# Another order of the SBUF buffers in a fp32 transformer kernel of two blocks

## The reference

```python
def swiglu(x, w_gate, w_up, w_down):
    return (jax.nn.silu(x @ w_gate) * (x @ w_up)) @ w_down      # 1024 -> 2816 -> 1024

for l in range(2):
    h = rmsnorm(x, ffn1_norm[l])
    x = x + 0.5 * swiglu(h, ffn1_w_gate[l], ffn1_w_up[l], ffn1_w_down[l])
    h = rmsnorm(x, mix_norm[l])
    p = h @ w_in[l]
    ...
    x = x + jnp.concatenate([y_pool, y_four, y_attn], axis=-1) @ w_out[l]
    h = rmsnorm(x, ffn2_norm[l])
    x = x + 0.5 * swiglu(h, ffn2_w_gate[l], ffn2_w_up[l], ffn2_w_down[l])
```

## Time and profile before

| | us |
|---|---|
| median of 3 runs | 2531.75 |
| lowest and highest run | 2531.56, 2534.13 |
| span of the profiled execution | 2529.9 |
| TensorE busy | 2457.5 |
| GpSimd busy | 1122.4 |
| VectorE busy | 1134.4 |
| ScalarE busy | 1082.3 |

### The profile page before, as it was taken

One profiled execution on the slowest core, in us unless ns is written; L12 is line 12 of the kernel. 1 busy time (PEld: TensorE's weight loads), 2 busy tenths in 40 slices (PEclk: granted clock), 3 DMA queues, 4 the chain that ended last, 5 costly groups with the idle time before them and its releaser, 6 DMA issues.

```text
span 2529.9 us, 30096 instructions
## 1 busy us (share of the span) xinstructions
PE 2457.5 (97%) x10934; PEld 1924.6 (76%) x10934; DVE 1134.4 (45%) x1780; ACT 1082.3 (43%) x1584; POOL 1122.4 (44%) x828
## 2 busy tenths in 40 slices
PE   8999999989999999999999989999999998999988
PEld 6888888667888888888888668888887665676666
DVE  5444115564444105444025655444136655465553
ACT  4333124454333214333132544333125777357772
POOL 4554445415455445554445414554445232352323
PEclk9999999999999999999999999999999999999999
DMA  4222223202222222222223203222233222122212
GB/s 172 85 97 99 100 88 128 84 34 100 99 99 88 95 100 92 91 99 99 100 83 129 73 32 110 90 98 99 100 119 104 83 80 67 67 96 75 84 63 83
DMA packets 37528, 233.17 MB, mean 92 GB/s; under 512 B 5184, under 2 KB 5312, under 8 KB 10816
## 3 DMA queue, kind: packets, MB, share of 16 engines
q1 hardware_dynamic: 36000, 226.51, 25.9%
q10 hardware_dynamic: 1440, 5.45, 0.6%
HBM read 223.55 MB, written 2.10 MB: 89 GB/s over the span
## 4 chain that ended last, share of the span: by engine, by line
issue 58%; POOL 41%; POOLq 1%
POOL w_lo L437 41%; POOLq L431 0%; POOLq L435 0%; POOLq L212 0%; POOLq L437 0%; POOLq L1874 0%
## 5 line engine op out<-in xcount | busy, mean ns | idle before, releaser
L437 POOL TENSOR_TENSOR w_lo<-raw,w_hi 128x512 fp32r<-128x512 f32 x824 | 1122.2, 1394 | 1406.9 <-ACT w_hi L924 1406.8
L445 PE MATMUL ps<-h_hi,w_hi 128*128 128x512 f32 x2304 | 921.3, 400 | 14.0 <-DVE h_lo L1330 7.9
L447 PE MATMUL ps<-h_hi,w_lo 128*128 128x512 f32 x2304 | 900.3, 391 | 0.0
L446 PE MATMUL ps<-h_lo,w_hi 128*128 128x512 f32 x2304 | 899.2, 390 | 0.0
L924 ACT ACTIVATE w_hi<-raw 128x1024 fp32r<-128x1024 f32 x412 | 413.3, 1052 | 881.2 <-PE ps L447 877.0
L445 PEld LDWEIGHTS ps<-h_hi,w_hi 128*128 128x128 f32 x2304 | 434.5, 189 | 115.7 <-issue 13.8
L446 PEld LDWEIGHTS ps<-h_lo,w_hi 128*128 128x128 f32 x2304 | 434.6, 189 | 93.5 <-issue 6.0
L447 PEld LDWEIGHTS ps<-h_hi,w_lo 128*128 128x128 f32 x2304 | 433.7, 188 | 92.2
L447 PE MATMUL ps<-hid_hi,w_lo 128*128 128x512 f32 x704 | 278.1, 395 | 0.0
L445 PE MATMUL ps<-hid_hi,w_hi 128*128 128x512 f32 x704 | 278.1, 395 | 0.0
L446 PE MATMUL ps<-hid_lo,w_hi 128*128 128x512 f32 x704 | 278.1, 395 | 0.0
(11 more groups left out here) (236 smaller groups left out, 2083.6 us busy)
## 6 DMA issues: line engine op xcount, KB each, us to landing
raw<-in_stream SPq DMA_DIRECT2D x206, 1024.0 KB, 4.8
hraw<-xs SPq DMA_DIRECT2D x96, 64.0 KB, 2.0
x_sb<-in_x SPq DMA_DIRECT2D x4, 512.0 KB, 10.5
out_x<-x_sb SPq DMA_DIRECT2D x8, 256.0 KB, 2.7
mem_sb<-in_mem ACTq DMA_DIRECT2D x1, 1024.0 KB, 10.2
rec_sb<-in_recip ACTq DMA_DIRECT2D x2, 512.0 KB, 4.6
memn<-in_mem ACTq DMA_DIRECT2D x1, 1024.0 KB, 4.8
dist_sb<-in_dist ACTq DMA_DIRECT2D x2, 448.0 KB, 3.1
```

What stands on the lines that cost most here:

```text
L437: gp.tensor_tensor(w_lo[:, s, c], raw[:, s, c], w_hi[:, s, c].bitcast(F32), ALU.subtract).then_inc(lo_split, 1)
L445: pe.matmul(dst, l_hi, r_hi, start=first, stop=False)
L446: pe.matmul(dst, l_hi, r_lo, start=False, stop=False)
L447: return pe.matmul(dst, l_lo, r_hi, start=False, stop=last)
```

## The change

The program text of the placement is turned round. The stacks of the shared stage buffers are entered first. Since they are all closed again, a tensor "region" of the size of the hidden layer's two parts (90,112 bytes, as much as any stage needs) is entered behind them to hold their range; nothing reads or writes it. Then come w_hi and w_lo, h_hi and h_lo, x_sb, raw and the small tensors. No instruction, wait, semaphore or loop is changed, and on every engine the instructions stand in the same order as before. Line numbers in the changed kernel are one higher from the PSUM tensor on.

```diff
-        x_sb = sb("x_sb", [P, KB, T])
-        h_hi = sb("h_hi", [P, KB, T], F32R)
-        h_lo = sb("h_lo", [P, KB, T], F32R)
-        raw = sb("raw", [P, 2, PANEL])
-        w_hi = sb("w_hi", [P, 2, PANEL], F32R)
-        w_lo = sb("w_lo", [P, 2, PANEL], F32R)
-        cst = sb("cst", [P, NC])
...
         ffn = ExitStack()
         hid_hi = sb("hid_hi", [P, FB, T], F32R, ffn)
         hid_lo = sb("hid_lo", [P, FB, T], F32R, ffn)
...
         two.close()
+        sb("region", [P, 2 * FB * T])
+        w_hi = sb("w_hi", [P, 2, PANEL], F32R)
+        w_lo = sb("w_lo", [P, 2, PANEL], F32R)
+        h_hi = sb("h_hi", [P, KB, T], F32R)
+        h_lo = sb("h_lo", [P, KB, T], F32R)
+        x_sb = sb("x_sb", [P, KB, T])
+        raw = sb("raw", [P, 2, PANEL])
+        cst = sb("cst", [P, NC])
...
```

More of the change, by code:

```diff
@@ L304, in build, with const @@
         two.close()
+        sb("region", [P, 2 * FB * T])
[6 more added lines that the diff above has]
+        cst = sb("cst", [P, NC])
+        vec_sb = sb("vec_sb", [P, LAYERS * (NV1 + NV2) + KB + 8])
+        v1_all = vec_sb[:, 0:LAYERS * NV1]
+        v2_all = vec_sb[:, LAYERS * NV1:LAYERS * (NV1 + NV2)]
+        fin_g = vec_sb[:, LAYERS * (NV1 + NV2):LAYERS * (NV1 + NV2) + KB]
+        lam_sb = vec_sb[0:64, LAYERS * (NV1 + NV2) + KB:LAYERS * (NV1 + NV2) + KB + 8]
+        fin_sq = sb("fin_sq", [P, KB])
+        fin_g2 = sb("fin_g2", [P, KB])
+        nlam_all = sb("nlam_all", [P, LAYERS])
+        mem_rstd = sb("mem_rstd", [P, 256])
+        scale2 = sb("scale2", [P, T])
+        eps2 = sb("eps2", [P, T])
+        sq = sb("sq", [P, 2, T])
+        ms = sb("ms", [P, 2, T])
+        guess = sb("guess", [P, 2, T])
+        newt = sb("newt", [P, 2, T])
+        hraw = sb("hraw", [P, 2, T])
+        mx = sb("mx", [P, 2, 2])
+        nmx = sb("nmx", [P, 2, 2])
+        ssum = sb("ssum", [P, 2, 2])
+        rsum = sb("rsum", [P, 2, 2])
+        tok_rstd = sb("tok_rstd", [P, TB])
+        tick = sb("tick", [P, 2])
+        eps = cst[:, NC - 1:NC]
+        def const(i):
+            return cst[:, i * P:(i + 1) * P]
         ps = ctx.enter_context(nc.psum_tensor("ps", [P, 8, 512], F32))
```

## The result

The changed kernel takes 2519.32 us at the median of four runs (2517.30 to 2521.43), the kernel before 2531.65 us (2530.05 to 2534.13, four runs). The ratio is 0.9948 with a 95% interval of 0.9936 to 0.9961: 12.3 us faster, which is rival A and not the forecast.

A forecast was written before the change was run, and what follows sets the result against it. TensorE, busy 97% of the span, was taken as the bound, through its matmul pace. All terms were 0: 2529.9 us of span plus 1.85 us from span to run median gave 2531.8 us, range 2515 to 2566.

The forecast's parts named there:

- rival A: TensorE's split matmuls on hid get h's pace through matching low address bits: 2517.6 us; chance 0.28, whole or part.
- Part 1: All engines and SP's queue: same instructions, waits, semaphores and order, none added; cost 0.
- Parts 2 to 4: ScalarE's writes, VectorE's subtractions, GpSimd's split, raw loads and TensorE's fp32 transposes: new places cost 0.
- Part 5: TensorE's split matmuls on hid and h: change of pace taken as 0, with ends -14.2 and +32.1 us.
- I take 0, which is nearest to the rows on mh and f: Choice for the split matmuls: mh's and f's spacings taken as evidence against a place effect; size 0.
- what would show it: List of signs per rival; for faster hid: its median falls to 389, h's stays, down parts 3.5 us shorter each.
- Rival B: Upper part of a partition slower for TensorE, so h slows and hid gains: 2563.9 us; chance 0.18.
- Rival D: Shifted meetings of VectorE with GpSimd's work: 2 us either way, counted inside the no-effect case, no chance of its own.

The follow-up runs named there:

- the first experiment: The kernel before with one unused tensor of 128 bytes ahead of the stage buffers, hid staying in the upper part: 2517.92 us, ratio 0.9946.

## Why the prediction was wrong

1. **Part 1** (no instruction changes): right, 30,096 instructions in both.
2. **Parts 2 to 4** (ScalarE, VectorE and fp32 transposes at 0): right within 1 ns.
3. **Part 5** failed, in the step "I take 0, which is nearest to the rows on mh and f". The term that was put at 0 measured -14.0 us. It was sized correctly as an end of the range (14.2 us), and the reason for it was named, the equal remainders of h and w. But the evidence against it was weighed wrongly in four places. mh has 256 columns, and there an offset doesn't lengthen the step (118.7 and 119.9 ns in the two layers at hid's offset, 119.9 in both without one), so its rows said nothing on 512. The six matmuls on f follow a pause, and f's step is 229.9 ns in the changed kernel too, where f agrees with the weights, against 230.8 before; its slowness has another reason. That h steps slowly just behind hid was read as "a stream that has just begun is slow whatever it reads"; but behind the fast hid h has 226 to 227 ns from its first step, at all three places where it follows, so those slow steps came with the slow hid ahead of them. And hid differed from h in two ways that the change leaves alone (the distance of the two parts, and eight banks with six matmuls each), which I took for as likely as the address; the first experiment keeps both and gets the gain, so neither sets the pace.
4. **Rival A** is what happened: 2517.6 us given, 2519.3 measured, with hid's median at 389 and h's unchanged, as "what would show it" said. It had 0.28.
5. **Rival B** is refuted in both directions, by h's pace at 124,032 and by hid's at 128,128.
6. **Rival D**: waits and the meetings of VectorE and GpSimd didn't move (1549 against 1548 ns in rows 8's terms).
7. By the two sections quoted no layout could change the time. That TensorE never waits for another engine at SBUF (the Trainium skill, "SBUF — State Buffer", "Who interferes with whom") isn't touched: the up part, with 43 us of VectorE in 90.7, and the down part, with none, have one pace after the change. That the gap follows from the columns alone, as in the formula for an isolated gap (the Trainium skill, "TensorE: Matmul & The Clock Gate", "Back-to-back issue gap"), is refuted for these split matmuls: 226.7 and 233.3 ns at 512 columns, by address.

The measured time lies in the range only because this reached to rival A; as a forecast of no change it was wrong.

## What to carry to other kernels

Where one form of matmul has two paces in one trace, compare the addresses of its operands first, and give a difference that is exact and instant more weight than rows of another width or of short streams. For split fp32 matmuls of 512 columns, place the moving tiles and the weights so that their byte offsets in a partition agree modulo 256; a small unused tensor ahead of a group of buffers does it (128 bytes in the first experiment). Here the agreement is worth 14 us on 2112 matmuls, and losing it on h as well cost another 32 us. A change of another buffer's size can turn this on or off, so look at the built addresses after every such change.

## What the runs showed that I had not expected

- A moving tile whose address differs from the weights' modulo 256 bytes lengthens the step of a 512-column split matmul from 226.67 to 233.33 ns, 16 cycles of the 2.4 GHz at which TensorE ran (granted clock 1.00). 32, 64 or 128 bytes short of the weights cost the same as 128 past them, 256 costs nothing, and the place in the partition doesn't matter.
- With only w_lo off, two of three matmuls pay: the one that uses it and the one beside which it is loaded.
- At 256 columns offsets don't lengthen the step: 119.9 ns a layer without one, and between 113.5 and 120.1 with one of 32, 64 or 128 bytes.
- hid's steady step was 232.4 and 233.3 ns in two layouts in which it and the weights have equal addresses, and behind a slow hid the first steps on h are slow (230 to 233 ns) where they are 227 behind a fast one.

What inside the chip makes the 256 bytes stays open: the runs show the relation, not its cause.
